# A two-block transformer kernel: the first loads are cut and ordered otherwise, and the variance ahead of the second up projection goes from VectorE and GpSimd to ScalarE

## What is computed

```python
h = rmsnorm(x, norm_mix); proj = h @ w_in              # the first product of the program
...
x = x + z            # z: g_post_mix * gate * rmsnorm(mixer output), second block
h2 = rmsnorm(x)      # needs mean(x*x) over all 2048 columns of each token
u = modulate(h2) @ w_ffn_in                            # the second up projection
...
x = x + gate * rmsnorm(ffn output)                     # the end of the program
```

## Time and profile before

| | |
|---|---|
| median of 3 runs | 2708.75 us (2708.39 to 2709.26) |
| the profiled execution | 2708.2 us, its span 2706.4 us, 1.8 us outside the span |
| PE busy | 2694.2 us |
| DVE, ACT, POOL busy | 2108.8, 855.3, 313.3 us |
| granted clock of PE over the span | 0.999 |

### The profile page before, as it was taken

One profiled execution on the slowest core, in us unless ns is written; L12 is line 12 of the kernel. 1 busy time (PEld: TensorE's weight loads), 2 busy tenths in 40 slices (PEclk: granted clock), 3 DMA queues, 4 the chain that ended last, 5 costly groups with the idle time before them and its releaser, 6 DMA issues.

```text
span 2706.4 us, 27691 instructions
## 1 busy us (share of the span) xinstructions
PE 2694.2 (100%) x9692; PEld 1725.8 (64%) x9692; DVE 2108.8 (78%) x3069; ACT 855.3 (32%) x1970; POOL 313.3 (12%) x495
## 2 busy tenths in 40 slices
PE   9999999999999999999999999999999999999998
PEld 8888888886444444444447888888444444444487
DVE  7988887987999999988887677886866667664444
ACT  2455555332453534530046442321321211111000
POOL 2112231000111111010101012100010010100000
PEclk9999999999999999999999999999999999999999
DMA  9888777677676677678775655555577676656554
GB/s 280 247 264 254 252 235 233 207 235 235 217 224 218 214 219 221 216 238 274 255 272 168 175 167 141 148 185 157 172 222 219 213 222 217 187 164 202 174 174 132
DMA packets 277660, 571.88 MB, mean 211 GB/s; under 512 B 26056, under 2 KB 27420, under 8 KB 277008
## 3 DMA queue, kind: packets, MB, share of 16 engines
q1 hardware_dynamic: 244384, 460.05, 54.8%
q0 software_dynamic: 32704, 109.73, 12.7%
q10 hardware_dynamic: 432, 0.34, 0.0%
HBM read 565.91 MB, written 4.11 MB: 211 GB/s over the span
## 4 chain that ended last, share of the span: by engine, by line
PE 85%; issue 14%; DVE 0%; POOLq 0%; POOL 0%; DVEq 0%; ACT 0%; ACTq 0%
PE PS L651 44%; PE PS L636 37%; PE PS L665 0%; PE PS L602 0%; PE PS L933 0%; PE PS L774 0%; PE PS L800 0%; PE PS L1003 0%; PE PS L986 0%; PE PS L696 0%; PE PS L722 0%; PE PS L805 0%; PE PS L779 0%; PE PS L862 0%; POOL mem L2575 0%
## 5 line engine op out<-in xcount | busy, mean ns | idle before, releaser
L1108 DVE TENSOR_TENSOR sums<-ring 128x512 f32<-128x512 f32 x429 | 301.0, 702 | 413.4 <-PE PS L651 257.6
L651 PE MATMUL PS<-sums,mem 128*128 128x512 f32 x1100 | 561.7, 592 | 0.0
L636 PE MATMUL PS<-ring,mem 128*128 128x256 f32 x1936 | 543.8, 380 | 0.1
L636 PE MATMUL PS<-sums,mem 128*128 128x256 f32 x1792 | 533.0, 379 | 0.0
L651 PE MATMUL PS<-ring,act_t 128*128 128x512 f32 x1056 | 510.7, 592 | 0.2 <-issue 0.2
L651 PE MATMUL PS<-ring,mem 128*128 128x512 f32 x880 | 438.6, 592 | 0.0
L636 PEld LDWEIGHTS PS<-ring,mem 128*128 128x128 f32 x1936 | 365.8, 190 | 52.1 <-issue 2.6
L651 PEld LDWEIGHTS PS<-sums,mem 128*128 128x128 f32 x1100 | 208.9, 190 | 262.6 <-issue 262.6
L636 PEld LDWEIGHTS PS<-sums,mem 128*128 128x128 f32 x1792 | 340.5, 190 | 46.3
L651 PEld LDWEIGHTS PS<-ring,act_t 128*128 128x128 f32 x1056 | 200.3, 190 | 250.6 <-issue 247.0
L2019 ACT COPY first_q<-PS 128x256 f32<-128x256 f32 (+1 forms) x73 | 32.5, 445 | 1020.8 <-PE PS L651 669.5
(11 more groups left out here) (302 smaller groups left out, 1927.6 us busy)
## 6 DMA issues: line engine op xcount, KB each, us to landing
ring<-in_w_in SPq DMA_DIRECT2D x240, 512.0 KB, 4.1
mem<-in_w_mod POOLq DMA_DIRECT2D x192, 512.0 KB, 4.7
ring<-in_w_up SPq DMA_DIRECT2D x176, 512.0 KB, 4.4
ring<-in_w_ffn_in SPq DMA_DIRECT2D x176, 512.0 KB, 4.5
ring<-in_w_down SPq DMA_DIRECT2D x88, 512.0 KB, 5.0
ring<-in_w_ffn_out SPq DMA_DIRECT2D x88, 512.0 KB, 3.8
ring<-in_w_out SPq DMA_DIRECT2D x64, 512.0 KB, 3.7
ring<-in_w_branch_a SPq DMA_DIRECT2D x16, 512.0 KB, 4.0
```

Of the source, the lines that this page charges most:

```text
L636: mm = pe.matmul(product(g, j), of(j, 2 * (c if part is None else part) + q), weights(j, n, q), start=lead and opens, stop=tail, skip_grou ...
L651: mm = pe.matmul(product(g, j), of(j, c), weight[j], start=lead, stop=tail, skip_group_check=True)
L1108: ve.tensor_tensor(one, b11, b12, ADD).then_inc(s["sums_ready"], 1)
```

## The change

**Loads.** x's first 512 columns come in one load (512 KB), in place of two of 256 columns. Then come the left halves of the two weight blocks (256 KB each), then the right halves. PE turns both pieces of x first, then the 4 turns of ones, then Q1 and Q2 of both halves, and turns pieces 2 and 3 only between `behind` of the two halves.

**Variance.** ACT adds the sums of squares (`plus`: an ACTIVATE on one column) and makes the variance. POOL keeps the maximum with EPS and the powers. DVE's eight small operations go; x's first addition stands ahead of the second wait. PE's 15 turns of ones become 8, a wait for POOL's first `rs2`, and 3. The additions in `half_squares` and `post_rstd` change at the end of the program too.

```diff
-            for q, (x_in, w_in_) in enumerate(((s["x_first"], s["w_first"]), (x_loaded[0], loaded[0]))):
-                cols_ = slice(T * q, T * q + T)
-                sp.dma_start(x_tok[:, :, cols_], x_halves[:, :, cols_]).then_inc(x_in, 16)
-                sp.dma_start(ring[:, 0, q, :, :], w_in[:, 2 * q:2 * q + 2, 0:CN]).then_inc(w_in_, 16)
+            sp.dma_start(x_tok[:, :, 0:CN], x_halves[:, :, 0:CN]).then_inc(x_loaded[0], 16)
+            for q in range(2):
+                sp.dma_start(ring[:, 0, q, :, 0:T], w_in[:, 2 * q:2 * q + 2, 0:T]).then_inc(w_ahead[q], 16)
+            for q, w_in_ in enumerate((s["w_first"], loaded[0])):
+                sp.dma_start(ring[:, 0, q, :, T:CN], w_in[:, 2 * q:2 * q + 2, T:CN]).then_inc(w_in_, 16)
...
                         norm_piece("mix", 0, None)
+                        norm_piece("mix", 1, None)
                         turns_of_ones(4)
-                        pe.wait_ge(s["w_first"], 16)
-                        pe.wait_ge(norm_sems["mix"]["kept"], 1)
-                        ahead(G0["proj"], n, c, 0, of_x)
-                        norm_piece("mix", 1, None)
+                        for q in range(2):
+                            pe.wait_ge(w_ahead[q], 16)
+                            pe.wait_ge(norm_sems["mix"]["kept"], q + 1)
+                            ahead(G0["proj"], n, c, q, of_x)
                         weights_in(pe, n)
-                        pe.wait_ge(norm_sems["mix"]["kept"], 2)
-                        ahead(G0["proj"], n, c, 1, of_x)
-                        norm_pieces("mix", 2, 4, None)
                         pe.wait_ge(s["forms_mix"], 1)
                         pe.wait_ge(s["sums_first"], 1)
                         behind(G0["proj"], n, c, 0, of_x)
+                        norm_pieces("mix", 2, 4, None)
...
             turns_of_ones(8, 2)
-            pe.wait_ge(s["var_ready"], 1)
-            turns_of_ones(7, 2)
+            pe.wait_ge(norm_sems["ffn2"]["rstd"], 1)
+            turns_of_ones(3, 2)
...
-            var_half(0)
-            var_half(1)
...
+            first_add(0)
             first_tile(0)
+            first_add(1)
+            x_add(mix_out, 0, slice(T, 2 * T))
             first_tile(1)
-            x_add_tile(1)
+            x_add(mix_out, 1, slice(T, 2 * T))
+            ve.drain()
+            norm_tok("ffn2", x_tok, ffn2_tmp, 1)
...
+            def plus(to, src, term, factor=1.0):
+                act.activation(to, src, ACT.Identity, scale=factor, bias=term)
+                act.drain()
+
+            def variance(h):
+
+                one = slice(h, h + 1)
+                z, xz = z_part[:, 6 + h:7 + h], xz_part[:, 6 + h:7 + h]
+                plus(z, z, z_pre[:, one])
+                act.wait_ge(s["post_dotted"], 4 + h)
+                plus(xz, xz, xz_pre[:, one])
+                act.wait_ge(s["post_rs"], 1 + h)
+                plus(half_v[:, one], z, xz, norm_rs[:, one])
+                plus(var2[:, one], half_v[:, one], x_ms[:, one], norm_rs[:, one])
+                act.drain().then_inc(s["var_ready"], 1)
...
                     square(buf[:, h, from_:upto], to, total)
+                    if free % 2:
+                        act.wait_ge(s["pre_summed"], k + 1)
+                        plus(total, total, ss_pre[:, h:h + 1])
+                    else:
+                        plus(total, total, part_ss[:, 6 + h:7 + h])
                     act.drain().then_inc(s["post_squared"], 1)
                     if k == 0 and free % 2 == 0:
                         act.wait_ge(s["post_scaled"], 4 + h)
                         square(mix_out[:, h, 3 * CN:D], to, z_part[:, 6 + h:7 + h])
-                        act.drain().then_inc(s["z_squared"], 1)
+                        variance(h)
...
                 for h, one in ((0, slice(0, 1)), (1, slice(1, 2))):
-                    pool.wait_ge(s["post_squared"], 7 * m + 4 + 2 * h)
-                    pool.tensor_tensor(ss_pre[:, one], ss_pre[:, one], part_ss[:, 6 + h:7 + h], ADD)
-                    pool.drain()
                     pool.wait_ge(s["post_squared"], 7 * m + 5 + 2 * h)
-                    pool.tensor_tensor(norm_rs[:, one], ss_pre[:, one], ss_last[:, one], ADD)
-                    pool.drain()
-                    pool.tensor_tensor(norm_rs[:, one], norm_rs[:, one], minus_half[:, one], ALU.pow)\
+                    pool.tensor_tensor(norm_rs[:, one], ss_last[:, one], minus_half[:, one], ALU.pow)\
                         .then_inc(s["post_rs"], 1)
...
+                    if m == 0:
+                        pool.wait_ge(s["var_ready"], h + 1)
+                        pool.tensor_scalar(var2[:, one], var2[:, one], EPS, None, ALU.max)
+                        pool.drain()
+                        pool.tensor_tensor(rs2[:, one], var2[:, one], minus_half[:, one], ALU.pow)\
+                            .then_inc(norm_sems["ffn2"]["rstd"], 1)
```

More of the change, by code:

```diff
@@ L298, in build @@
         x_loaded = [sem(f"x_loaded{n}") for n in range(4)]
+        w_ahead = [sem(f"w_ahead{n}") for n in range(2)]
         names = [
@@ L682, in norm_piece @@
                 if key == "mix":
-                    pe.wait_ge(x_loaded[j // 2] if j else s["x_first"], 16)
+                    pe.wait_ge(x_loaded[j // 2], 16)
                 else:
@@ L1268, in _ @@
             combine_pair(act_t, ext_x, 1, "forms_mix")
+            ve.wait_ge(w_ahead[1], 16)
             weights_in(ve, 0)
@@ L1866, in dot_half @@
                                         accum_out=xz_part[:, 6 + h:7 + h])
-                ve.drain()
-            def var_half(h):
-                one = slice(h, h + 1)
-                ve.wait_ge(s["post_rs"], 1 + h)
-                ve.wait_ge(s["z_squared"], 4 + h)
-                ve.scalar_tensor_tensor(half_v[:, one], z_pre[:, one], z_part[:, 6 + h:7 + h], norm_rs[:, one], ADD, MUL)
-                ve.drain()
-                ve.scalar_tensor_tensor(half_v[:, one], xz_pre[:, one], xz_part[:, 6 + h:7 + h], half_v[:, one], ADD, ADD)
-                ve.drain()
-                ve.scalar_tensor_tensor(var2[:, one], half_v[:, one], norm_rs[:, one], x_ms[:, one], MUL, ADD)
-                ve.drain()
-                ve.tensor_scalar(var2[:, one], var2[:, one], EPS, None, ALU.max).then_inc(s["var_ready"], 1)
+                ve.drain().then_inc(s["post_dotted"], 1)
             ve.wait_ge(s["post_squared"], 2)
@@ L1890, in _, with first_add @@
             dot_half(1)
-            var_half(0)
-            var_half(1)
+            def first_add(h):
+                ve.wait_ge(s["post_rs"], h + 1)
+                x_add(mix_out, h, slice(0, T))
+                ve.drain()
             def first_tile(h):
                 cols = slice(0, T)
-                x_add(mix_out, h, cols)
-                ve.drain()
                 ve.wait_ge(norm_sems["ffn2"]["rstd"], h + 1)
@@ L1900, in first_tile @@
                     .then_inc(norm_sems["ffn2"]["tok"], 1)
-            def x_add_tile(j):
-                for h in range(2):
-                    x_add(mix_out, h, slice(T * j, T * (j + 1)))
-                ve.drain()
-                norm_tok("ffn2", x_tok, ffn2_tmp, j)
             def ffn2_turn(k):
```

13 lines of the change are left out of this document (4 added, 9 removed).

## The result

| | before | changed |
|---|---|---|
| median of 22 runs | 2708.84 us (2708.18 to 2709.39) | 2712.89 us (2710.32 to 2714.59) |
| ratio | | 1.0015, 95% interval 1.0010 to 1.0021 |
| profiled execution | 2708.2 us, span 2706.4 | 2712.54 us, span 2710.7 |

The changed kernel takes 4.05 us, 0.15%, longer. That is within the 0.2% named as no change, but the forecast was 0.2 us less, with 2710.4 as its upper end: the time lies 2.5 us above the range, and the sign is wrong. The runs also scatter over 4.3 us, where those of the kernel before scatter over 1.2.

The account below looks back on a forecast made before the run. PE was taken as the bound, busy 2694.2 of 2706.4 us. Start +0.65, ahead of up2 -0.8 and end -0.05 sum to -0.2 us on a median of 2708.75: 2708.55, stated as 2708.6, range 2707.6 to 2710.4.

Parts of the forecast that it names:

- ACT's small operations: Ahead of up2, each `plus` on ACT was taken at 0.27 us, with bounds of 0.20 to 0.35.
- part two: Variance ahead of up2: half 1's products start 1.07 us earlier, and the place gains 0.8 us, at best 1.0.
- What bounds the kernel: PE, busy 2694.2 of 2706.4 us; the change touches three places: the start, ahead of up2, and the end.
- x lands later: At the start, the first turn of x comes 0 to 0.6 us later, taken as 0.3; x lands at 5.1 at the latest.
- The first `behind`: At the start, DVE's first combinations end at 9.8 in place of 9.50; PE, through at about 9.1, idles until 9.85.
- The turns of pieces 2 and 3: At the start, they begin 1.85 us later, DVE's chunk 1 sums come late, and the start loses 0.65 us.
- rival (c): PE's clock falls in the longer wait ahead of up2 and returns late, losing 2 us: 2710.6; chance 0.07.
- POOL's powers: Ahead of up2, POOL's power was taken at 0.55 us, as DVE only waits there; 0.98 was seen beside DVE's product.
- rival (b): The variance change ahead of up2 gains nothing, ACT's small operations costing 0.35 and a power 0.98: 2709.4; chance 0.12.
- the turns that fall away: Ahead of up2, the 4 turns of ones removed cost nothing and give nothing, as PE waits after them.
- The rule of large loads: At the start, four weight loads paid one after another at 2.6 us each would lose some 5 us; the trace speaks against it.

Follow-up runs that it names:

- e5_turns_ahead: `e1_start_only` with pieces 2 and 3 turned ahead of the products that wait for DVE: 2709.12 us, +0.67 against the kernel before.
- e17_mended: Changed kernel with 10 ones ahead of x, pieces 2 and 3 turned ahead, and 12 ones in the long wait: 2709.1 us, +0.6 against the kernel before.
- e1_start_only: Kernel before with only the change's loads and its order at the start, variance left on DVE: 2711.29 us, +2.2.
- e12_start_filled: `e1_start_only` with 10 first turns of ones in place of 7: 2709.83 us, +1.4 against the kernel before.
- e10_variance_filled: `e2_variance_only` with 12 turns of ones in the wait ahead of half 1's turn before up2: 2709.16 us, +0.8 against the kernel before.
- e2_variance_only: Changed kernel with the loads and the start of before, so only the variance is changed: 2711.81 us, +2.7 against the kernel before.
- e4_no_fill: Kernel before without its 15 turns of ones ahead of up2, nothing else changed: 2711.32 us, +2.25.
- e1: Short for `e1_start_only`: kernel before with only the change's loads and start order, 2711.29 us, +2.2.
- e5: Short for `e5_turns_ahead`: `e1_start_only` with pieces 2 and 3 turned earlier, 2709.12 us, +0.67 against the kernel before.
- e15: Kernel before with 4 turns of ones at the start in place of 7, adding a wait ahead of x: 2709.66 us, +1.15.
- e16: Kernel before with 5 turns of ones at the start in place of 7, adding a wait ahead of x: 2708.94 us, +0.4.
- e13_gains_first: `e12_start_filled` with the gains' load issued ahead of the identity's on ACT's queue: 2710.93 us, +2.6 against the kernel before.
- e8_x_and_left_by_turns: Kernel before's variance, with loads alternating x's 256-column pieces and left weight halves, pieces 2 and 3 turned before `behind`: 2708.59 us, +0.1.

## Why the prediction was wrong

Two steps failed above all. The price of ACT's small operations was too low, which turned part two from a gain of 0.8 us into a loss of 0.7 to 0.8; and PE's clock was given no term in the sum, neither behind the longer wait ahead of up2 (1.4 to 2.4 us) nor behind the wait for x at the start (up to 0.8). The order of the turns was foreseen as a loss, at half its size.

**The balance.** Chain at the start 1.4 us (nearly all of it the turns' order, by `e5_turns_ahead` and `e17_mended`); clock at the start up to 0.8 (`e1_start_only` less `e12_start_filled`); chain ahead of up2 0.8; clock there 1.9; end 0. These add up to 4.9, and 4.05 was measured; the terms are differences of medians whose runs scatter by 2 us and hold the late weight load in unknown parts. The changed kernel's profile, by positions, has 1.35 at the start, 0.8 of that load, 0.7 chain and 1.4 clock ahead of up2: 4.3 us.

**What bounds the kernel** was read rightly: all of the change lay in three short places, and the one other place that moved, at 1640 us, moves in the kernel before too.

**x lands later.** The step "I take 0.3" for a range of 0 to 0.6 failed: x landed at 5.2, just beyond the upper end of 5.1, and PE's first turns are 0.77 us later, at 5.34. The premise that a double row costs less than two pieces has no support in any profile with this load (x landed at 5.1 to 5.7).

**The gains** were in no step. I had read SP's queue and not ACT's, whose two small loads share the DMA engines with SP's. The chain of waits in the changed kernel's profile begins with the 5.24 us of one of them, but it cost some 0.35 us there at most (6.46 against the estimated 6.10).

**The first `behind`**: a wait of 0.7 us ahead of 9.85 was forecast, 0.97 ahead of 10.37 came. DVE's first combinations ended at 10.24 in place of 9.8, by x and the gains. (A fourth of the step from 9.27 to 10.21 is 0.235 and not 0.22; nothing hangs on it.)

**The turns of pieces 2 and 3.** This mechanism was right in each step: they begin 2.24 behind the product (forecast 2.2), DVE idles 1.81 (1.8), PE then waits 0.88 for chunk 1's sums (0.65), and chunk 2 adds nothing (24.55 against 23.19, 1.36 late, and 1.29 at chunk 1). Its size was 1.3 in place of 0.65, since it inherited the lateness of the first combinations. What I failed to do is to put a cost on the clock at the start: the "0.3 us at 4.8" of rival (c) was a wait of 0.6 to 0.75 us before the clock had risen.

**ACT's small operations.** The step "I take 0.27 each" failed, and so did its upper bound of 0.35: start to start they take 0.36 to 0.45 us within a chain, and on average 0.43. It was built from a Square of one column (0.20) and a drain of 0.07 that no row of ACT shows, where the rows show 0.29 (0.39 with a column as scale too) and 0.44 from a single `plus` to the next instruction. Twelve of them lie ahead of the second power. The last two were to be done 3.9 us behind the products and were done at 5.2, and POOL's power at 6.2 in place of 4.8. From a gain of 0.7 at the turn of half 1 it became a loss of 0.8.

**POOL's powers** were right: 0.56 with DVE still (0.55 forecast). Beside a working DVE, half 0's took 0.98.

**The clock ahead of up2** was rival (c), with a chance of 0.07, and came true as it was described: the granted clock falls behind the wait, and the price of 2 us is what `e10_variance_filled` and `e2_variance_only` show (1.9). Its chance was too low for a plain reason. It hung on how long the wait is, this hung on the term for `plus`, and that term had no row of its own. Its bounds were also worked out too kindly: with 0.35 each, and a power of 0.98, my own sum puts half 1's turn 1.2 us later than forecast, and part two loses 0.3 us, where I wrote that all of the gain is lost; rival (b) should have stood at 2709.7. And the new order removed the second block of ones (7 turns behind the first half's signal) at the place where the wait grew; I had written that the turns that fall away "cost nothing and give nothing".

**The loads.** The rule of large loads, weighed against the trace, did not decide: the four halves landed at 6.30, 7.04, 7.83 and 8.54, 0.7 to 0.8 us apart, and nobody waited for them. The working by the rule was wrong besides. The 2.0 us stand in the page's section on the anatomy of one DMA, for loads issued by GpSimd, and the change adds two weight loads and saves one of x, so paid one after another they would be 2 us (4 for the weights alone), not 5.

## What to carry to other kernels

Where PE waits for a chain, a longer chain costs twice if the wait grows past what the clock bears: keep useless products in the wait until the real ones can start, and lengthen them with the chain. Before moving work on PE behind products that wait for another engine, ask which engine needs the moved work's output next. Small operations should be priced by a row from start to start with their drain, and a small load at the start by when it lands among the large ones, whatever queue it is on.

## What the runs showed of the hardware that I had not expected

- An ACTIVATE on one column with a column as bias takes 0.29 us, with a column as scale too 0.39; with their drains the steps in a chain are 0.36 and 0.45, and four of them hold ACT for 1.71.
- PE bore a wait of 1.28 us ahead of up2 with the clock at 1.00 throughout, and not one of 3.05 (granted clock 0.72 behind it), 3.10 or 4.97. The half clock lasted 3.3 us or more in the first profile (1906.80 to 1910.10) and 6.8 us in the other two (1903.20 to 1910.00 in `e2_variance_only`, 1900.80 to 1907.60 in `e4_no_fill`).
- At the start a wait of 0.7 to 1 us, before the clock has risen, put off the rise by some 3 to 5 us in the profiles of `e1`, `e5`, `e15` and `e16`; by the runs it does so in some executions only. The scatter of the runs shows it better than the median: 2.8 us (`e16`) against 0.7 us for a start without it (`e12_start_filled`).
- Loads of 8 and 64 KB, issued second on ACT's queue beside the change's loads of SP's, landed 5.2 and 5.7 us after their issue; beside the loads of before the 8 KB took 3.1 to 4.6 us, and issued first in `e13_gains_first` 2.6. The same identity load landed at 5.5 us in one execution and at 6.9 in another.
- The first load of x, 256 KB, landed at 4.3 us in the profile of before, at 4.1 in that of `e15` and at 4.8 in that of `e16`, with the same loads in all three, so the 5.1 us of `e8_x_and_left_by_turns`, where only what is queued behind it differs, is little beyond their spread. What sets the spread stays open.
